# GpSimd's subtraction for the weights' low parts, cut from one instruction per tile into four

## The chip, the cores and the metric

The kernel runs on one core of one Trainium2 chip. The metric is the device time of one execution in microseconds (us). Before the change it is 1412.34 us, the median of three runs (1410.88 to 1412.73).

A core has five engines that run side by side and wait for each other by semaphores: TensorE (PE in the profile; PEld is its weight load), VectorE (DVE), ScalarE (ACT), GpSimd (POOL) and SyncE (SP), which only issues transfers here.

## The reference

256 positions of 1024 channels pass through three transformer layers. Cut to the products that matter here:

```python
# layer 1
mod = silu(c) @ ada_w + ada_b
proj = (rmsnorm(x) * (1 + sc1) + sh1) @ w_in          # 1024 x 3624
mix = concat([hgrn2_mixer(..), dsa_mixer(..), conv_module(..)]) @ w_out
x = x + g1 * mix
ff = square(relu(h @ mlp_w1)) @ mlp_w2                # 1024 x 4096, 4096 x 1024
x = rmsnorm(x + g2 * ff)
# layers 2 and 3
x = layer_norm(ALPHA * x + mixer(x))                  # MLA and stick-breaking, then "fox"
x = layer_norm(ALPHA * x + (silu(x @ w1) * (x @ w3)) @ w2)   # inner width 2816
x = x + sigmoid(x @ ple_w_gate + b) * (p @ ple_w_proj)
```

All data are float32.

## The kernel before

**Weights as a stream.** Every weight matrix is cut on the host into tiles of at most 128 x 2048 (1 MB), in the order in which TensorE uses them (`STREAM`). SyncE loads them into a ring of three buffers, `raw`. The 24 tiles `ada*` are multiplied as they are (line 569). Each of the other 159 (`SPLIT`) is made into two rounded parts, so that a float32 product is three fast ones:

- ScalarE copies `raw` to `w_hi` in the rounded type (line 949, inside `ahead`, called two tiles ahead between its other work). There are three `w_hi` buffers.
- GpSimd subtracts: `w_lo = raw - w_hi` (line 1279, inside `remainder`). There are two `w_lo` buffers. 155 of the tiles have 2048 columns; the others have 1088, 256, 1536 and 128.
- TensorE's `product3` (lines 491, 496 and 497) adds `a_hi*b_hi`, `a_hi*b_lo` and `a_lo*b_hi` in PSUM.

The activations are split in the same way by VectorE: at the start of a stage `split_input` makes `hT_hi` (a cast, line 1344) and `hT_lo` (a subtraction, line 1345), in four chunks of 512 columns; in the first MLP lines 1677 to 1679 square, cast and subtract each half of the hidden layer, and in the two later ones lines 1882 to 1887 do two multiplications, a cast and a subtraction per pair of tiles.

**Who waits for whom.** GpSimd starts tile n when ScalarE has rounded it and TensorE has finished the first product of tile n-1, since only then is the `w_lo` buffer of tile n-2 free:

```python
pool.wait_ge(weights_rounded, n + 1)
if n >= LO:
    pool.wait_ge(weights_started, n - LO + 2)
```

TensorE waits for the whole tile (`pe.wait_ge(weights_split, n + 1)` in `tile`) before its first product of it. So GpSimd cannot work ahead: from one tile's first product to the next tile's first product there must be time for one whole subtraction. The same semaphore, `weights_split`, lets SyncE overwrite the `raw` buffer.

**Stages.** A product with 1024 inputs takes one tile for 256 outputs: 48 products of 256 columns (`feature_half`, `token_half`). The down projections (`down`, 16 tiles in the first MLP, 11 in each of the other two) have 24 products of 512 columns per tile. The first MLP's up projection has 16 tiles (`m1`), the two others 22 each (`f13`, two tiles per step). In the stage of the gated recurrence (VectorE's lines 1498 to 1529, eight levels) GpSimd also computes a convolution of 31 taps, each a multiplication (line 1290) and an addition (line 1292) of 512 columns, with a wait behind each, and puts the subtractions of four tiles between the first taps; from the last instruction of such a tile to the next tap's multiplication there is no wait.

At the end of the layers 2 and 3 comes the stage with the embedding product (`pp`) and the gate products (`pg`).

Of the kernel before, what the change touches and what calls it, by code (L numbers as in the profile page):

```python
# [23 lines left out]
F32 = mybir.dt.float32  # L24
ALU = mybir.AluOpType
# [9 lines left out]
RAW, HI, LO = 3, 3, 2  # L35
# [43 lines left out]
def width(name):  # L79
    return WIDTH.get(name, TILE)  # L80
# [175 lines left out]
def bank(*key):  # L256
    return USE[key] % BANKS


def read(*key):  # L260

    return USE[key] // BANKS + 1


def build(nc, x_in, wstream, pcol_in, prow_in, const_in, p_in, out):
    ctx = ExitStack()
    with ctx:
        def sb(name, shape):
            return ctx.enter_context(nc.sbuf_tensor(name, shape, F32))

        def sem(name):
            return ctx.enter_context(nc.semaphore(name))
# [6 lines left out]
        def rounded(name, n, offset=None):  # L279

            if offset is None:
                return ctx.enter_context(nc.sbuf_tensor(name, [P, n], F32R))
            return nc.alloc_sbuf_tensor_at(name, [P, n], F32R, offset=arena_at + 4 * offset)

        raw = sb("raw", [P, RAW, TILE])
        w_hi = [rounded(f"w_hi{i}", TILE) for i in range(HI)]
        w_lo = [rounded(f"w_lo{i}", TILE) for i in range(LO)]
# [25 lines left out]
        def col(name, i=0, n=1):  # L313
            return pcol[:, PCOL[name] + i:PCOL[name] + i + n]
# [90 lines left out]
        weights_split = sem("weights_split")  # L405
# [40 lines left out]
        @block.sync  # L446
        def _(sp):
            for i, name in enumerate(STREAM):
                if i >= RAW:
                    before = STREAM[i - RAW]  # L450
                    if before in SPLIT_NO:
                        sp.wait_ge(weights_split, SPLIT_NO[before] + 1)
                    elif int(before[3:]) % 2 == 0:
                        sp.wait_ge(ada_used, int(before[3:]) // 2 + 1)
                    else:
                        sp.wait_ge(psum_full, full("mod", int(before[3:]) // 2))
                sp.dma_start(raw[:, i % RAW, 0:width(name)], wstream[i, :, 0:width(name)])\
                    .then_inc(weights_loaded[i % RAW], 16)
            sp.wait_ge(x_done, 1)
            sp.dma_start(out.rearrange("o (t p) d -> p (o t) d", p=P), x[:, :, :])\  # L460
                .then_inc(out_stored, 16)
            sp.wait_ge(out_stored, 16)
# [800 lines left out]
        @block.gpsimd  # L1263
        def _(pool):
            step = [0]

            def link(ins):
                step[0] += 1
                ins.then_inc(pool_step, 1)
                pool.wait_ge(pool_step, step[0])  # L1270

            def remainder(name):

                n, slot = SPLIT_NO[name], TILE_NO[name]
                pool.wait_ge(weights_rounded, n + 1)
                if n >= LO:
                    pool.wait_ge(weights_started, n - LO + 2)
                m = width(name)
                nc.gpsimd.tensor_tensor(w_lo[n % LO][:, 0:m], raw[:, slot % RAW, 0:m],  # L1279
                                        w_hi[n % HI][:, 0:m].bitcast(F32), ALU.subtract).then_inc(weights_split, 1)  # L1280

            hp = hpad.rearrange("p (c n) -> p c n", c=2)
            acc = conv.rearrange("p (c n) -> p c n", c=2)

            def tap(j):


                product_ = mixT[:, 4 + 2 * (j % 2):6 + 2 * (j % 2), :]
                w = col("cv_w", 2 * j, 2).unsqueeze(2).to_broadcast([P, 2, T])
                link(nc.gpsimd.tensor_tensor(product_, hp[:, :, j:j + T], w, ALU.mult))  # L1290
                before = col("cv_b", 0, 2).unsqueeze(2).to_broadcast([P, 2, T]) if j == 0 else acc
                last = nc.gpsimd.tensor_tensor(acc, product_, before, ALU.add)
                if j < 30:
                    link(last)
                else:
                    last.then_inc(conv_done, 1)

            for name in SPLIT[:SPLIT_NO["hg.0"]]:
                remainder(name)
            pool.wait_ge(pcol_loaded, 16)  # L1300
            pool.wait_ge(bank_read[bank("cu", 0)], read("cu", 0))
            for j in range(31):
                tap(j)

                if j % 2 == 0 and SPLIT_NO["hg.0"] + j // 2 < SPLIT_NO["wo0.0"]:
                    remainder(SPLIT[SPLIT_NO["hg.0"] + j // 2])
            for name in SPLIT[SPLIT_NO["wo0.0"]:]:
                remainder(name)
# [738 lines left out]
```

## Time and profile before

| | |
|---|---|
| median of three runs | 1412.34 us (1410.88 to 1412.73) |
| span of the profiled execution, first to last instruction | 1405.2 us |
| median less that span | 7.1 us |
| TensorE, busy share | 85% |
| VectorE, busy share | 52% |
| ScalarE, busy share | 37% |
| GpSimd, busy share | 58% |
| line 1279: 159 instructions, busy | 731.3 us |
| mean granted TensorE clock | 0.918 of full speed |

"Busy" includes time in which an instruction has started and is held up. The times of the profiled execution are given from the start of its span; of its own time the profile has the span alone, so the work around it is read from the median.

### The profile page before, as it was taken

Reading aid. Unit: us, or ns where it says so; the run is one execution under the profiler, and the core shown is the slowest. Engines: PE = TensorE matmul, PEld = TensorE weight load, DVE = VectorE, ACT = ScalarE, POOL = GpSimd, SP = SyncE. Lnnn points to the kernel's source line nnn. Section 1 sums busy time; section 2 is a strip of 40 time slices with the busy share of each in tenths; the row PEclk is TensorE's granted clock in tenths of the full one; section 3 lists DMA queues with packets and bytes.
Section 4 is the critical chain, followed back from the end, with each engine's and each line's share of the span. In section 5 each row is a group of like instructions: output and inputs, shape, how many; then the busy total and the mean of one; then the engine's idle time right before and its main releaser. Section 6 shows DMA issues by size and latency. Waiting matters only on the chain.

```text
span 1405.2 us, 18835 instructions
## 1 busy us (share of the span) xinstructions
PE 1200.8 (85%) x8000; PEld 1104.7 (79%) x8000; DVE 727.2 (52%) x778; ACT 521.1 (37%) x672; POOL 813.5 (58%) x225
## 2 busy tenths in 40 slices
PE   6699769576999996975779999976999788999976
PEld 5699658466998885973679999866987488999866
DVE  2396999656999005336555553074022536555054
ACT  1453210433343333456433333333554433333341
POOL 0476896133877882740157878844743146888863
PEclk9899879868999997997799999988999889999998
DMA  9442218412444554330034455524432033455540
GB/s 363 167 175 90 91 36 302 172 44 106 164 167 174 185 183 161 139 129 1 31 120 150 181 180 182 207 92 165 181 120 90 0 120 130 191 186 184 181 148 30
DMA packets 28131, 200.95 MB, mean 143 GB/s; under 512 B 3089, under 2 KB 3473, under 8 KB 4881
## 3 DMA queue, kind: packets, MB, share of 16 engines
q1 hardware_dynamic: 26624, 190.30, 37.0%
q10 hardware_dynamic: 1424, 9.46, 1.8%
q8 instruction: 63, 1.03, 0.3%
q14 instruction: 20, 0.16, 0.0%
HBM read 198.70 MB, written 1.05 MB: 142 GB/s over the span
## 4 chain that ended last, share of the span: by engine, by line
PE 68%; DVE 20%; ACT 5%; issue 4%; DMA 1%; POOL 1%; DVEq 0%; ACTq 0%; POOLq 0%
PE bank L491 19%; PE bank L496 18%; PE bank L497 18%; PE bank L569 6%; DVE hT_hi L1344 4%; DVE hT_lo L1345 3%; DVE arena L1677 2%; PE bank L620 2%; DVE hid_lo L1679 2%; DVE arena L1529 1%; PE bank L613 1%; DVE hid_hi L1678 1%; PE bank L857 1%; PE bank L856 1%; POOL w_lo L1279 1%
## 5 line engine op out<-in xcount | busy, mean ns | idle before, releaser
L1279 POOL TENSOR_TENSOR w_lo<-raw,w_hi 128x2048 fp32r<-128x2048 f32 (+1 forms) x159 | 731.3, 4600 | 569.6 <-PE bank L491 489.2
L949 ACT ACTIVATE w_hi<-raw 128x2048 fp32r<-128x2048 f32 (+1 forms) x159 | 299.6, 1886 | 342.1 <-PE bank L491 288.2
L491 PE MATMUL bank<-hT_hi,w_hi 128*128 128x256 f32 (+1 forms) x1360 | 392.1, 288 | 35.1 <-DVE hT_lo L1345 30.1
L496 PE MATMUL bank<-hT_lo,w_hi 128*128 128x256 f32 (+1 forms) x1360 | 389.3, 286 | 0.0
L497 PE MATMUL bank<-hT_hi,w_lo 128*128 128x256 f32 (+1 forms) x1360 | 389.1, 286 | 0.0
L491 PEld LDWEIGHTS bank<-hT_hi,w_hi 128*128 128x128 f32 (+1 forms) x1360 | 264.3, 194 | 39.7 <-DVE hT_lo L1345 20.3
L496 PEld LDWEIGHTS bank<-hT_lo,w_hi 128*128 128x128 f32 (+1 forms) x1360 | 264.2, 194 | 0.2
L497 PEld LDWEIGHTS bank<-hT_hi,w_lo 128*128 128x128 f32 (+1 forms) x1360 | 263.7, 194 | 0.3
L491 PE MATMUL bank<-w_hi,hT_hi 128*128 128x256 f32 (+2 forms) x544 | 164.5, 302 | 35.0 <-DVE hT_lo L1345 29.0
L496 PE MATMUL bank<-w_lo,hT_hi 128*128 128x256 f32 (+2 forms) x544 | 161.8, 298 | 0.0
L497 PE MATMUL bank<-w_hi,hT_lo 128*128 128x256 f32 (+2 forms) x544 | 161.7, 297 | 0.0
L491 PEld LDWEIGHTS bank<-w_hi,hT_hi 128*128 128x128 f32 x544 | 113.5, 209 | 39.3 <-DVE hT_lo L1345 25.2
L491 PE MATMUL bank<-w_hi,hid_hi 128*128 128x512 f32 (+1 forms) x336 | 128.9, 384 | 1.8 <-POOL w_lo L1279 1.8
L496 PE MATMUL bank<-w_lo,hid_hi 128*128 128x512 f32 (+1 forms) x336 | 128.7, 383 | 0.0
L497 PE MATMUL bank<-w_hi,hid_lo 128*128 128x512 f32 (+1 forms) x336 | 128.5, 383 | 0.0
L496 PEld LDWEIGHTS bank<-w_lo,hT_hi 128*128 128x128 f32 x544 | 113.7, 209 | 0.2
L497 PEld LDWEIGHTS bank<-w_hi,hT_lo 128*128 128x128 f32 x544 | 113.4, 208 | 0.2
L569 PE MATMUL bank<-raw,tiny 128*128 128x256 f32 x384 | 88.0, 393 | 10.6 <-DVE tiny L1449 9.0
L1886 DVE CAST hid_hi<-arena 128x512 fp32r<-128x512 f32 x22 | 96.0, 4366 | 0.7
L569 PEld LDWEIGHTS bank<-raw,tiny 128*128 128x128 f32 x384 | 75.9, 198 | 22.6 <-DVE tiny L1449 9.0
L491 PEld LDWEIGHTS bank<-w_hi,hid_hi 128*128 128x128 f32 x336 | 64.4, 192 | 14.3 <-POOL w_lo L1279 2.3
L497 PEld LDWEIGHTS bank<-w_hi,hid_lo 128*128 128x128 f32 x336 | 64.2, 191 | 12.0
(242 smaller groups left out, 1347.0 us busy)
## 6 DMA issues: line engine op xcount, KB each, us to landing
raw<-wstream SPq DMA_DIRECT2D x179, 1024.0 KB, 4.8
arena<-prow ACTq DMA_DIRECT2D x2, 2560.0 KB, 8.9
x_res<-x ACTq DMA_DIRECT2D x1, 1024.0 KB, 12.4
rows<-prow ACTq DMA_DIRECT2D x2, 512.0 KB, 15.4
out<-x_res SPq DMA_DIRECT2D x1, 1024.0 KB, 4.0
const_sb<-const ACTq DMA_DIRECT2D x1, 936.0 KB, 14.2
raw<-wstream SPq DMA_DIRECT2D x1, 768.0 KB, 4.1
raw<-wstream SPq DMA_DIRECT2D x1, 544.0 KB, 3.6
```

Of the source, the lines that this page charges most:

```text
L491: ins = mm(o, a[0], b[0], start=start, stop=False)
L496: mm(o, a[0], b[1], start=False, stop=False)
L497: return mm(o, a[1], b[0], start=False, stop=stop)
L569: last = mm(b[:, j * T:(j + 1) * T], csil[:, k:k + 1].to_broadcast([P, P]), w[:, k, :], start=k == 0, stop=k == DC - 1)
L620: last = mm(b[par * 64:par * 64 + 64, hh * P:(hh + 1) * P], values(4 * g + par + 2 * hh, m), pT_[:, (hh * nb + m) * P:(hh * nb + m + 1) * ...
L949: A(w_hi[n % HI][:, 0:m], raw[:, slot % RAW, 0:m], ACT.Copy).then_inc(weights_rounded, 1)
L1279: nc.gpsimd.tensor_tensor(w_lo[n % LO][:, 0:m], raw[:, slot % RAW, 0:m], w_hi[n % HI][:, 0:m].bitcast(F32), ALU.subtract).then_inc(weights ...
L1344: link(V.tensor_copy(hT_hi[:, s], src))
L1345: V.tensor_tensor(hT_lo[:, s], src, hT_hi[:, s].bitcast(F32), ALU.subtract).then_inc(input_split, 1)
L1677: link(V.tensor_tensor(v, act_out[n % 2], act_out[n % 2], ALU.mult))
L1679: V.tensor_tensor(hid_lo[:, hs], v, hid_hi[:, hs].bitcast(F32), ALU.subtract).then_inc(hid_split, 1)
L1886: link(V.tensor_copy(hid2_hi[:, hs], v))
```

## The change

In `remainder` the one subtraction of a tile becomes a loop. The step is 512 columns where the width is a multiple of 512, and a quarter of the width otherwise: four instructions per tile, but three of 512 for the one tile of 1536 columns. The four follow each other with no wait between them. The two waits stand before the first, and the semaphore `weights_split` is raised by the last. The tile's data and all other engines' instructions are the same. The line of the subtraction becomes 1281, and those below it move on by three.

```diff
                 m = width(name)
-                nc.gpsimd.tensor_tensor(w_lo[n % LO][:, 0:m], raw[:, slot % RAW, 0:m],
-                                        w_hi[n % HI][:, 0:m].bitcast(F32), ALU.subtract).then_inc(weights_split, 1)
+                step_ = 512 if m % 512 == 0 else m // 4
+                for c in range(0, m, step_):
+                    last = nc.gpsimd.tensor_tensor(w_lo[n % LO][:, c:c + step_], raw[:, slot % RAW, c:c + step_],
+                                                   w_hi[n % HI][:, c:c + step_].bitcast(F32), ALU.subtract)
+                last.then_inc(weights_split, 1)
```

## Rows read from the trace of the kernel before

**Rows 1.** The page: busy time of each engine, and the chain by engine.
```profile
PE 1200.8 (85%) x8000; PEld 1104.7 (79%) x8000; DVE 727.2 (52%) x778; ACT 521.1 (37%) x672; POOL 813.5 (58%) x225
...
PE 68%; DVE 20%; ACT 5%; issue 4%; DMA 1%; POOL 1%; DVEq 0%; ACTq 0%; POOLq 0%
```

**Rows 2.** Busy time by stretch: an up projection (f13), then its down projection.
```profile
core 0: us, PE busy (x) PEld busy (x) DVE busy (x) ACT busy (x) POOL busy (x), PEclk, DMA share, GB/s
735.00:870.00 135.00, 135.00 (x1083) 133.34 (x1083) 75.29 (x48) 49.40 (x34) 105.35 (x23) 0.99 0.49 178
870.00:922.00 52.00, 50.45 (x223) 41.43 (x221) 3.38 (x6) 18.75 (x11) 42.66 (x10) 1.00 0.52 185
```

**Rows 3.** Timeline of GpSimd: narrower tiles, and two tiles of a down projection.
```profile
start us, us, engine line op out<-in xcount [idle before <-releaser]
600.61 3.52 POOL L1279 TENSOR_TENSOR w_lo<-raw,w_hi 128x1536 fp32r<-128x1536 f32 x1 [1.14 <-PE bank L491]
...
960.48 0.46 POOL L1279 TENSOR_TENSOR w_lo<-raw,w_hi 128x128 fp32r<-128x128 f32 x1 [1.14 <-PE bank L491]
...
871.85 4.62 POOL L1279 TENSOR_TENSOR w_lo<-raw,w_hi 128x2048 fp32r<-128x2048 f32 x1 [0.81 <-PE bank L491]
877.31 4.62 POOL L1279 TENSOR_TENSOR w_lo<-raw,w_hi 128x2048 fp32r<-128x2048 f32 x1 [0.84 <-PE bank L491]
```

**Rows 4.** Timeline of GpSimd between tiles and taps, and VectorE beside it.
```profile
125.86 4.59 POOL L1279 TENSOR_TENSOR w_lo<-raw,w_hi 128x2048 fp32r<-128x2048 f32 x1
130.41 1.04 POOL L1290 TENSOR_TENSOR mixT<-arena,pcol_sb 128x512 f32<-128x512 f32 x1
...
136.08 4.89 POOL L1279 TENSOR_TENSOR w_lo<-raw,w_hi 128x2048 fp32r<-128x2048 f32 x1
140.91 1.50 POOL L1290 TENSOR_TENSOR mixT<-arena,pcol_sb 128x512 f32<-128x512 f32 x1
...
202.58 1.27 POOL L1292 TENSOR_TENSOR arena<-mixT,arena 128x512 f32<-128x512 f32 x1
...
136.40 5.12 DVE L1529 TENSOR_TENSOR arena<-arena 128x512 f32<-128x512 f32 x1
141.56 1.41 DVE L1498 TENSOR_TENSOR xn<-arena 128x512 f32<-128x512 f32 x1
```

**Rows 5.** Timeline of GpSimd and VectorE in the first up projection (m1).
```profile
355.57 5.08 POOL L1279 TENSOR_TENSOR w_lo<-raw,w_hi 128x2048 fp32r<-128x2048 f32 x1 [1.14 <-PE bank L491]
...
392.31 4.59 POOL L1279 TENSOR_TENSOR w_lo<-raw,w_hi 128x2048 fp32r<-128x2048 f32 x1 [3.12 <-ACT w_hi L949]
397.49 4.91 POOL L1279 TENSOR_TENSOR w_lo<-raw,w_hi 128x2048 fp32r<-128x2048 f32 x1 [0.59 <-PE bank L491]
...
355.48 0.69 DVE L1679 TENSOR_TENSOR hid_lo<-arena,hid_hi 128x512 fp32r<-128x512 f32 x1
356.21 5.00 DVE L1677 TENSOR_TENSOR arena<-arena 128x512 f32<-128x512 f32 x1
```

**Rows 6.** Waits of TensorE, 345 to 470 us: in total, times, longest.
```profile
PE bank L491 <- POOL w_lo L1279: 5.5, 4, 1.8
```

**Rows 7.** Timeline of GpSimd and VectorE in an up projection f13.
```profile
745.62 4.63 POOL L1279 TENSOR_TENSOR w_lo<-raw,w_hi 128x2048 fp32r<-128x2048 f32 x1 [1.14 <-PE bank L491]
...
746.18 4.34 DVE L1886 CAST hid_hi<-arena 128x512 fp32r<-128x512 f32 x1
750.56 0.69 DVE L1887 TENSOR_TENSOR hid_lo<-arena,hid_hi 128x512 fp32r<-128x512 f32 x1
```

**Rows 8.** Timeline of VectorE in the first input product, and in the residual behind the mixer.
```profile
87.76 3.44 DVE L1479 TENSOR_TENSOR arena<-arena 128x1024 f32<-128x1024 f32 x1 [0.69 <-ACT arena L1025]
91.24 9.05 DVE L1482 TENSOR_TENSOR_SCAN xn<-ones,arena 128x256 f32<-128x256 f32 x4
...
309.35 4.54 DVE L1662 TENSOR_TENSOR x_res<-x_res,arena 128x512 f32<-128x512 f32 x1
```

**Rows 9.** Timeline at the start of the up projection m1: GpSimd, then VectorE.
```profile
337.12 4.73 POOL L1279 TENSOR_TENSOR w_lo<-raw,w_hi 128x2048 fp32r<-128x2048 f32 x1 [12.27 <-PE bank L491]
...
337.50 4.63 DVE L1344 CAST hT_hi<-arena 128x512 fp32r<-128x512 f32 x1
...
343.35 0.69 DVE L1345 TENSOR_TENSOR hT_lo<-arena,hT_hi 128x512 fp32r<-128x512 f32 x1
```

**Rows 10.** Timeline at the start of layer 2's gate stage: GpSimd, VectorE, TensorE.
```profile
930.57 5.06 POOL L1279 TENSOR_TENSOR w_lo<-raw,w_hi 128x2048 fp32r<-128x2048 f32 x1 [10.55 <-PE bank L491]
936.74 4.76 POOL L1279 TENSOR_TENSOR w_lo<-raw,w_hi 128x2048 fp32r<-128x2048 f32 x1 [1.11 <-PE bank L491]
...
937.13 4.92 DVE L1345 TENSOR_TENSOR hT_lo<-arena,hT_hi 128x512 fp32r<-128x512 f32 x1
...
942.11 0.58 PE L491 MATMUL bank<-w_hi,hT_hi 128*128 128x256 f32 x1 [3.48 <-DVE hT_lo L1345]
```

## The prediction

> **What bounds the kernel now.** I read the busy times and the chain first, then stretches, then single rows. TensorE is busy 85% of the span and carries 68% of the chain that ended last; VectorE carries 20%, GpSimd 1% [rows 1]. In the up projections TensorE is never idle, and GpSimd is busy 105 of 135 us beside it; in the down projections it is close to the same [rows 2]. That "1%" is deceptive. GpSimd may not work ahead: tile n's subtraction starts behind the first product of tile n-1 and must end before tile n's. What matters is the room in that loop. In a down projection a tile comes about every 5.44 us: the subtraction takes 4.62 and GpSimd idles 0.81 [rows 3]; in the wide products tiles come every 5.76 us (4.62 busy and 1.14 idle) [rows 5, 7]. How much of the idle time is room? At 397.49 us TensorE itself had waited for GpSimd, and still GpSimd was idle 0.59 us [rows 5]: that is the loop's own latency (the end of the subtraction, the first product, the next start). So the real room is 1.14 - 0.59 = **0.55 us** per tile in wide products and about **0.2 us** in down projections.
>
> The second thing to see is that GpSimd and VectorE hold each other up. A cast of 512 columns takes 4.34 us when a subtraction of GpSimd started before it [rows 7], a two-input operation of 0.69 us takes 5.00, and a subtraction that starts while VectorE's is running takes 5.08 instead of 4.62 [rows 5]. One of them has to end before the other goes on. The blocked VectorE operation that began at 356.21 ends at 361.21, 0.56 after GpSimd's end at 360.65, so its 0.69 began 0.13 before that end; the other way round GpSimd loses 0.46. I take 0.14 us of overlap at each exchange.
>
> The Trainium skill (SBUF — State Buffer, "Who interferes with whom") calls this an exclusive lock, taken for a whole instruction by GpSimd or by a VectorE operation that has two SBUF inputs or uses both ports. The trace agrees (5.00 against 0.69).
>
> **Cost of a piece.** 128 columns take 0.46 us, 1536 take 3.52 and 2048 take 4.62 [rows 3]. That is 2.15 to 2.17 ns a column over a fixed 0.19, which gives 1.29 us for 512 columns; the convolution's addition of 512 columns takes 1.27 [rows 4]. I take 1.28. Of two instructions with no wait between them the second starts about 0.045 us before the first ends (125.86 + 4.59 = 130.45 against 130.41) [rows 4]. Four pieces take 4 x 1.28 - 3 x 0.045 = **4.99 us**, 0.37 more than now. Bounds: nothing is added if a piece's fixed part vanishes behind its neighbour (1.15, a quarter of 4.62), and 1.32 a piece if the slope from the 1536-column tile is carried down.
>
> On that price the Trainium skill (GPSIMD Engine Reference, "Performance pitfalls for Q7 kernels") speaks against the change: a read command costs about 102 cycles that do not overlap with the previous one. As an estimate, three more instructions with one to two such reads are 0.26 to 0.51 us a tile, 4.88 to 5.13 in all; by the upper one the result would be some 9 us later than mine. No row here shows it apart.
>
> **Does VectorE get in between pieces?** At 140.91 GpSimd's tap follows the tile at once. A VectorE subtraction was waiting and got in: it ended at 141.52, and the tap took 1.50 us instead of 1.04. At 130.41, with nobody waiting, the same tap took 1.04 [rows 4]. So yes, by the nearest row, at the end of every instruction. A two-input operation in a gap costs GpSimd 0.46, a cast (0.43 us) 0.43 - 0.28 + 0.045 = 0.20.
>
> **The sum, where it costs:**
> - Down projections: 4.99 + 0.60 = 5.59 us per tile against 5.44. Some 35 intervals (15 + 10 + 10) x 0.15 = **+5.3**.
> - f13: in every second tile a cast and a subtraction now enter between the pieces: 4.99 + 0.20 + 0.46 = 5.65, and with 0.59 a period of 6.24 against 5.76. Nothing can be made up, as GpSimd can't work ahead. 22 steps x 0.48 = **+10.6**. The other tile of each step (4.99 + 0.59 = 5.58) still fits.
> - m1: three operations per tile (0.46, 0.20, 0.46). When TensorE falls behind, the first of them lands in the 0.59 between two tiles, wholly or partly, so a tile takes 5.65 to 6.1 and the period is 6.24 to 6.7; I take 6.37. 16 x 0.61 = 9.8. Against it stands what m1 loses now: VectorE, blocked for a whole tile at a time, falls behind, ScalarE then rounds late (3.12 us of idle at 392.31 [rows 5]), and TensorE waits 5.5 us [rows 6]. That wait goes. Together **+4.3**.
> - First input product: the subtraction of 1024 columns and the four scans [rows 8] enter between pieces of three tiles, some 0.8 over the period each, an estimate from 0.46 apiece: **+2.5**.
> - Residual behind the mixer: three tiles with one operation each [rows 8], 4.99 + 0.46 + 0.59 - 5.76 = 0.28: **+0.9**.
>
> **Where it pays:**
> - Gate stages, twice. VectorE's last subtraction waits behind the second tile until 942.05, and TensorE 3.48 us for it [rows 10]. Now the first tile really starts at 931.0 (5.06 - 4.62 late); its pieces alternate with cast, subtraction, cast: 4 x 1.28 + 1.55 - 6 x 0.14 = 5.83, end at 936.85; the last subtraction ends at 937.4. The wait of 3.48 goes, but TensorE gets the tile 0.6 later than now: 2 x 2.9 = **-5.8**.
> - Other stage starts, eight. The cast is blocked for 4.2 us, but behind it stand three more operations, and all of them alternate with pieces now. From the real start at 337.23: 5.83 + 0.55 gives 343.6 for the last, against 344.04 now [rows 9]. 8 x 0.4 = **-3.2**. So the most visible stalls give back next to nothing.
> - Recurrence: VectorE's work at 136.40 is blocked 4.4 us [rows 4], and there are four such tiles, at most 4 x 3.3 = 13. But each tile ends some 1.8 us later, and the products hg.1 and hi.1 and the exponentials behind them are waited for. Taking the order through piece by piece with the prices above leaves **-3**; the bounds are 0 and -10.
>
> Everything that only unblocks VectorE elsewhere costs and gives nothing, as TensorE covers it; without that cover VectorE's operations would count. The loads cost nothing: a `raw` buffer comes free at the end of its subtraction, as now, just before the tile's first product, so its reload keeps a whole period.
>
> Sum: 5.3 + 10.6 + 4.3 + 2.5 + 0.9 - 5.8 - 3.2 - 3.0 = **+11.6 us**. The sum is made against the profiled span of 1405.2, which gives 1416.8; with the 7.1 us between that span and the median (an unprofiled 1412.34) that is **1424 us**.
>
> **Rivals.**
> - *Pieces are nearly free and the stalls shrink* (faster). If GpSimd prepares a piece while the one before streams, four take about 4.65. Down projections then lose nothing, f13 0.5 in all, m1 is even, the first product loses 1.5, the residual nothing, and the gains of 12 stay: -10, **1402**. It decides below about 1.245 us a piece. For it: the overlap of 0.045 shows some preparation. Against: the fixed 0.19 is still in the tap behind a tile. Chance 0.19.
> - *The ends cancel*, with pieces of 1.24 to 1.26: **1412**, chance 0.08.
> - *GpSimd keeps its place through its four pieces.* Then VectorE is blocked for 4.99 instead of 4.62: down +5.3, m1 +7.5 (VectorE falls further behind), stage starts and recurrence 10 x 0.37 = 3.7 and no gains: about +16, **1428**. Against: the row at 140.91. Chance 0.12.
> - *A piece costs over 1.35*, since dispatch shows between short instructions. At 1.40, a tile takes 5.47 + 0.59 = 6.06, and all of about 100 wide tiles run late: +0.3 each, the mixed ones and the down projections more: some +53, **1465**. No row of 512 columns is that long unblocked. Chance 0.05.
> - *The forecast itself*, 0.56.
>
> **The numbers.** A measurement of this kernel can tell about 0.2% (2.8 us) from no change. Faster takes the first rival, 0.19; within 0.2% 0.09, the cancelling case and an edge; slower the rest, 0.72. With 1.25 a piece the sum is some +2, with 1.32 some +21. The range, 1405 to 1436 us, leaves out the far end of the dispatch case and the lower part of the first rival.
>
> **What would show it.** 512-column pieces of 1.27 to 1.29 us, starts 1.24 apart; down projections with periods near 5.59; f13 periods of 5.76 and 6.2 in turn, and waits of TensorE for GpSimd of some 0.5 us there; in m1 the late rounding gone; VectorE's longest operations near 1.7 us instead of 5; the 3.48 us before the gate product gone. Wrong: periods of 5.44 in the down projections (pieces cheaper), or VectorE's casts still over 4 us (no entry between pieces).

## The result and the profile after

The changed kernel takes **1440.26 us** (median of 4 runs, 1439.02 to 1445.19) against 1412.53 for the kernel before beside it (4 runs, 1410.88 to 1413.70): a ratio of 1.0208, 95% interval 1.0188 to 1.0228. A second measurement in the study gave 1442.93 against 1407.22, ratio 1.0243 (1.0218 to 1.0268). The forecast was 1424, with a range up to 1436: the sign was right and the size was not. The change costs 28 to 36 us where the sum had 11.6. The ratios are estimated apart from the medians, with their intervals, and can differ slightly from the ratio of two medians.

The profiled execution took 1445.19 us, its span 1443.4, and TensorE's mean granted clock was 0.911 of full speed (0.918 before). First the page of the changed kernel: the busy times and the chain by engine, as [rows 1].

```profile
PE 1234.3 (86%) x8000; PEld 1112.6 (77%) x8000; DVE 599.6 (42%) x778; ACT 526.6 (36%) x672; POOL 930.8 (64%) x701
...
PE 57%; POOL 24%; DVE 11%; ACT 4%; issue 2%; DMA 1%; DVEq 0%; POOLq 0%; ACTq 0%
```

VectorE's busy time fell by 127.6 us, because it is blocked less, and GpSimd's rose by 117.3. On the chain GpSimd went from 1% to 24% and VectorE from 20% to 11%. VectorE was freed, and GpSimd became what TensorE waits for. The stretches that answer to [rows 2] (up projection f13, then its down projection):

```profile
core 0: us, PE busy (x) PEld busy (x) DVE busy (x) ACT busy (x) POOL busy (x), PEclk, DMA share, GB/s
752.00:887.00 135.00, 131.83 (x1046) 128.11 (x1046) 44.94 (x44) 50.30 (x34) 119.76 (x90) 1.00 0.46 166
887.00:939.00 52.00, 51.97 (x219) 40.07 (x218) 0.00 (x0) 17.55 (x10) 45.69 (x37) 1.00 0.51 185
```

In 135 us TensorE now does 1046 products instead of 1083, and in the 52 us of the down projection 219 instead of 223, with GpSimd busy 45.69 us where it was 42.66.

Now the places of the sum, in the program's order. Timeline of GpSimd in the first input product; then at the start of m1 (GpSimd, then VectorE), as [rows 9]; then in m1 (GpSimd, then VectorE), as [rows 5]:

```profile
start us, us, engine line op out<-in xcount [idle before <-releaser]
88.16 6.54 POOL L1281 TENSOR_TENSOR w_lo<-raw,w_hi 128x512 fp32r<-128x512 f32 x4 [0.59 <-PE bank L491]
95.28 6.92 POOL L1281 TENSOR_TENSOR w_lo<-raw,w_hi 128x512 fp32r<-128x512 f32 x4 [0.59 <-PE bank L491]
...
339.37 6.01 POOL L1281 TENSOR_TENSOR w_lo<-raw,w_hi 128x512 fp32r<-128x512 f32 x4 [11.36 <-PE bank L491]
...
339.77 1.40 DVE L1347 CAST hT_hi<-arena 128x512 fp32r<-128x512 f32 x1
344.30 1.64 DVE L1348 TENSOR_TENSOR hT_lo<-arena,hT_hi 128x512 fp32r<-128x512 f32 x1
...
358.27 5.76 POOL L1281 TENSOR_TENSOR w_lo<-raw,w_hi 128x512 fp32r<-128x512 f32 x4 [0.59 <-PE bank L491]
364.62 6.08 POOL L1281 TENSOR_TENSOR w_lo<-raw,w_hi 128x512 fp32r<-128x512 f32 x4 [0.59 <-PE bank L491]
...
358.52 1.41 DVE L1681 CAST hid_hi<-arena 128x512 fp32r<-128x512 f32 x1
359.97 1.67 DVE L1682 TENSOR_TENSOR hid_lo<-arena,hid_hi 128x512 fp32r<-128x512 f32 x1
```

A row with x4 is a whole tile. VectorE's casts and two-input operations of 512 columns that were held up for 4.3 to 5.0 us [rows 5, 7, 9] now take 1.40 (a cast) or 1.64 to 1.67 (two inputs): they wait for one piece. And each one that gets in makes the tile longer, with GpSimd idle just 0.59 us around it, so that the loop itself sets the pace.

Timeline of GpSimd in an up projection f13, as [rows 7], and in its down projection, as [rows 3]:

```profile
758.55 5.67 POOL L1281 TENSOR_TENSOR w_lo<-raw,w_hi 128x512 fp32r<-128x512 f32 x4 [0.70 <-PE bank L491]
764.81 5.06 POOL L1281 TENSOR_TENSOR w_lo<-raw,w_hi 128x512 fp32r<-128x512 f32 x4 [0.59 <-PE bank L491]
...
885.40 5.05 POOL L1281 TENSOR_TENSOR w_lo<-raw,w_hi 128x512 fp32r<-128x512 f32 x4 [0.70 <-PE bank L491]
891.16 5.04 POOL L1281 TENSOR_TENSOR w_lo<-raw,w_hi 128x512 fp32r<-128x512 f32 x4 [0.71 <-PE bank L491]
```

The f13 tiles start 6.26 and 5.76 us apart in turn. In the down projection the tile's four pieces take 5.04 and the starts are 5.76 apart, not 5.59: the idle time is 0.70, where 0.60 was forecast. TensorE's own rows at the change of tile say why:

```profile
890.12 0.39 PE L497 MATMUL bank<-w_hi,hid_lo 128*128 128x512 f32 x1
890.50 0.50 PE L491 MATMUL bank<-w_hi,hid_hi 128*128 128x512 f32 x1
890.85 0.40 PE L496 MATMUL bank<-w_lo,hid_hi 128*128 128x512 f32 x1
```

Products of one tile start 0.23 us apart and take 0.39. The first product of a tile that TensorE had to wait for takes 0.50, and GpSimd may start on the next tile only behind it (it does at 891.16). The 0.59 of [rows 5] was read behind a late first product of 256 columns, in the kernel before:

```profile
396.96 0.39 PE L491 MATMUL bank<-hT_hi,w_hi 128*128 128x256 f32 x1 [1.34 <-POOL w_lo L1279]
```

That product takes 0.39 us, so the loop is 0.11 us longer with products of 512 columns.

Last, layer 2's gate stage (GpSimd, VectorE, TensorE), as [rows 10]:

```profile
952.34 6.29 POOL L1281 TENSOR_TENSOR w_lo<-raw,w_hi 128x512 fp32r<-128x512 f32 x4 [10.16 <-PE bank L491]
959.23 9.02 POOL L1281 TENSOR_TENSOR w_lo<-raw,w_hi 128x512 fp32r<-128x512 f32 x4 [0.59 <-PE bank L491]
...
959.22 3.47 DVE L1762 TENSOR_TENSOR x_res<-xn,arena 128x1024 f32<-128x1024 f32 x2
962.72 4.40 DVE L1765 TENSOR_TENSOR x_res<-x_res,arena 128x1024 f32<-128x1024 f32 x2
...
968.30 0.58 PE L491 MATMUL bank<-w_hi,hT_hi 128*128 128x256 f32 x1 [3.59 <-POOL w_lo L1281]
```

The wait of 3.48 us for VectorE is gone, as forecast, and a wait of 3.59 for GpSimd stands in its place, one tile later. Behind VectorE's last subtraction stand four residual updates of 1024 columns. TensorE's next products don't need them, but they get in between the pieces of the second tile and stretch it to 9.02 us.

**Stages.** The times below lie between the same ScalarE instructions in each trace, as a mean of two traces of the kernel before and two of the changed one (spans 1405.2 and 1411.0, 1443.4 and 1441.0; means 34.1 us apart).

| stage | forecast, us | measured, us |
|---|---|---|
| to the end of the first input product | +2.5 | +5.4 |
| recurrence, on to the output product of the mixer | -3.0 | -4.8 |
| that product and the start of m1 | +0.1 | -0.5 |
| m1 and its down projection | +6.6 | +9.1 |
| layer 2's mixer, to its first f13 step | -1.2 | +0.8 |
| layer 2's f13 and down projection | +6.8 | +8.8 |
| layer 2's gate stage, to layer 3's attention | -3.3 | +1.2 |
| layer 3's attention | 0 | +3.8 |
| from there to its first f13 step | -0.8 | +0.9 |
| layer 3's f13 and down projection | +6.8 | +9.1 |
| last gate stage to the end | -2.9 | +0.3 |
| sum | +11.6 | +34.1 |

The smallest of these differences are within what two traces of one kernel show: those of the kernel before lie 2.7 us apart in layer 2's mixer, and those of the change 3.1 us in the first input product (3.8 and 7.0 more than before).

### The profile page after: what moved, and what is told of

Same layout as the page of the kernel before. It is cut to its first block, busy times and chain, and to the rows that moved or that the text cites. A ratio compares the mean times of both kernels' runs of the same rounds, so it can differ in the third digit from the quotient of the medians.

```text
span 1443.4 us, 19311 instructions
## 1 busy us (share of the span) xinstructions
PE 1234.3 (86%) x8000; PEld 1112.6 (77%) x8000; DVE 599.6 (42%) x778; ACT 526.6 (36%) x672; POOL 930.8 (64%) x701
## 3 DMA queue, kind: packets, MB, share of 16 engines
q10 hardware_dynamic: 1424, 9.46, 1.7%
## 4 chain that ended last, share of the span: by engine, by line
PE 57%; POOL 24%; DVE 11%; ACT 4%; issue 2%; DMA 1%; DVEq 0%; POOLq 0%; ACTq 0%
POOL w_lo L1281 23%; PE bank L491 16%; PE bank L496 14%; PE bank L497 14%; PE bank L569 5%; DVE hT_lo L1348 3%; DVE hT_hi L1347 2%; PE bank L620 2%; PE bank L857 1%; PE bank L613 1%; PE bank L856 1%; DMA raw<-wstream 1%; PE bank L555 1%; POOL arena L1295 1%; POOL mixT L1293 1%
## 5 line engine op out<-in xcount | busy, mean ns | idle before, releaser
L1281 POOL TENSOR_TENSOR w_lo<-raw,w_hi 128x512 fp32r<-128x512 f32 x635 | 851.0, 1372 | 490.9 <-PE bank L491 427.0
L491 PE MATMUL bank<-hT_hi,w_hi 128*128 128x256 f32 (+1 forms) x1360 | 398.9, 293 | 44.0 <-DVE hT_lo L1348 26.8
L491 PE MATMUL bank<-w_hi,hid_hi 128*128 128x512 f32 (+1 forms) x336 | 132.7, 395 | 3.1 <-POOL w_lo L1281 3.0
L496 PEld LDWEIGHTS bank<-w_lo,hid_hi 128*128 128x128 f32 x336 | 63.7, 190 | 10.7
```

The source lines that it names most:

```text
L491: ins = mm(o, a[0], b[0], start=start, stop=False)
L496: mm(o, a[0], b[1], start=False, stop=False)
L1281: last = nc.gpsimd.tensor_tensor(w_lo[n % LO][:, c:c + step_], raw[:, slot % RAW, c:c + step_], w_hi[n % HI][:, c:c + step_].bitcast(F32), ...
```

## The experiments

In those that cut, the form is that of the change, and only the tiles that are cut and the widths differ. `COND` and `STEPS` are given with each; a tile outside `COND` keeps its one instruction.

```diff
-                nc.gpsimd.tensor_tensor(w_lo[n % LO][:, 0:m], ...).then_inc(weights_split, 1)
+                steps = STEPS if COND else [m]
+                c = 0
+                for s_ in steps:
+                    last = nc.gpsimd.tensor_tensor(w_lo[n % LO][:, c:c + s_], ...)
+                    c += s_
+                last.then_inc(weights_split, 1)
```

### The change by parts

**Down projections alone**, in pieces of 512:

```diff
+                COND: name[:2] in ('m2', 'f2')
```

> Only the 38 tiles of the down projections (m2, f2) are cut into four. VectorE works on nothing there, so this is the price of the cuts alone. Theory A (a piece has a fixed cost, and GpSimd's loop has no room): a tile takes 5.04 us instead of 4.62 and the period goes from 5.44 to 5.74, 38 x 0.30 = +11 us over the kernel before. Theory B (the cuts are nearly free and the 28 us come from VectorE's entries between pieces): within 2 us of the kernel before. Theory C (a lower granted clock makes the loss): no change of the period, and whatever is lost shows as a lower clock.

1420.52 us (1417.38 to 1425.27), ratio 1.0096 (1.0076 to 1.0117). Timeline of GpSimd in a down projection of this kernel:

```profile
890.07 5.04 POOL L1282 TENSOR_TENSOR w_lo<-raw,w_hi 128x512 fp32r<-128x512 f32 x4 [0.71 <-PE bank L491]
895.81 5.04 POOL L1282 TENSOR_TENSOR w_lo<-raw,w_hi 128x512 fp32r<-128x512 f32 x4 [0.70 <-PE bank L491]
```

VectorE does next to nothing in these stages, so this is the pure price of the cuts: a period of 5.74 us against 5.44 to 5.46, and +3.3, +3.7 and +3.7 us in the three down projections. That is 10.7 in all, some 0.30 for each of the 35 intervals, twice the forecast's 5.3.

**Up projections alone**, m1 and f13:

```diff
+                COND: name[:2] == 'm1' or name[:3] == 'f13'
```

> Only the 60 tiles of the up projections (m1, f13) are cut into four. Theory A: m1 periods of 6.54 us against 5.76, 16 x 0.78 = 12.5, less the 5.5 us that TensorE waits there now; f13 0.52 per step, 22 x 0.52 = 11.4; together +18 us. Theory B: the same, and it is then nearly all of the loss (over +24 us). Theory C: under +5 us.

1433.82 us (1422.46 to 1437.42), ratio 1.0169 (1.0133 to 1.0205). Its f13 tiles behave as in the whole change (ten intervals in 119.82 us against 119.81, and 115.20 before), so the two kinds of projection don't depend on each other there. m1 and its down projection take just 2.7 us more than before, where 7 were expected.

**All the others alone:**

```diff
+                COND: not (name[:2] in ('m1', 'm2', 'f2') or name[:3] == 'f13')
```

> The other 61 tiles alone are cut into four: the first input products, the tiles among the convolution's taps, the mixers' products and the gate stages. By the two traces: +6.9 us up to 112 us, -4.6 in the recurrence, -0.6 behind it, +1.6 in the two gate stages, some +0.6 elsewhere: +2 to +6 us. If the parts add up (theory A), the three runs sum to the 28 us of the whole change; if they don't, there is a loss that only the whole has. The prediction had a gain of 6.6 us for this part.

1418.39 us (1415.21 to 1420.57), ratio 1.0076 (1.0057 to 1.0096). Here lie all the places that should have paid back. Of these the recurrence does (144.4 us against 149.2), but the first input product takes nearly as much again (115.7 against 111.7).

The three ratios make 1.034 together, the change 1.021 to 1.024. Much of the difference lies in layer 3's attention, to which the study comes back below. With that stage taken out of each profiled span, the kernel before has 1378.6 us (mean of its two traces), and the parts 1391.3, 1394.5 and 1380.5, which is 12.7, 15.9 and 1.9 more and 30.5 in sum; the change has 1408.9 (mean of two), 30.3 more. So the totals add up, but not every stage does. m1 and its down projection take 3.3, 2.7 and -1.2 us more in the three runs, 4.8 in sum, and 9.1 more in the whole change. The starts of GpSimd's tiles show a part of it. From the down projection's second tile to the first tile behind it there are fifteen intervals. They take 85.4 us in the kernel before, because ScalarE's late rounding reaches into its first tiles, and 81.8 when m1 alone is cut, because that lateness is gone. With the down projection cut they take 87.3 us behind a late m1 (alone) and 86.8 behind a punctual one (the whole change). So the same cut costs 1.9 us in the one case and 5.0 in the other. What makes up for it in the other stages wasn't taken apart.

**Both kernels again**, with no edit to either, on the chip of the next two runs:

> The kernel before, once more, for a second profiled execution. The two traces at hand differ by 5.9 us in the attention of layer 3, where GpSimd has no tile in hand, and the granted clock there was 0.61 and 0.54 in the slices of the changed kernel and 1.00 in those of the kernel before. If that fall belongs to the executions and not to the change (theory D), this trace may show it too, and its stages other than that one agree with the first trace within 1 us. If it belongs to the change (theory C), the clock stays at 1.00 here, as before.

> The changed kernel, once more. Theory D: the stages with tiles lose what they lost in the first trace, +32 us without that attention stage, within 2 us, and the attention stage anything from 0 to +13. In the median against the kernel before: +25 to +32 us.

1407.76 us for the kernel before (ratio 1.0005, 0.9988 to 1.0023), and 1442.93 for the change. The first says that two measurements of one kernel agree within 0.3%; the second that the loss of 2 per cent and more stands on another chip too.

### Is it the cut, or who enters?

In f13 VectorE's cast and subtraction fall on every second tile. Cutting only those, or only the other ones, keeps the number of extra instructions and changes whether anybody gets in.

```diff
+                COND: name[:3] == 'f13' and name[-2:] == '.1'
```

> Only those 22 tiles of f13 are cut into four (the .1 of each step) that GpSimd subtracts while VectorE casts and subtracts. Theory A: a cut tile with two entries takes 5.7 us and the loop 0.59, so each step is 0.5 longer: +11 us over the two stages, read between the first and the last sigmoid of each. Theory B' (the price is in the cuts and not in the entries): about what f13_quiet costs.

```diff
+                COND: name[:3] == 'f13' and name[-2:] == '.0'
```

> Only the other 22 tiles of f13 (the .0 of each step) are cut into four; VectorE does nothing there that holds GpSimd up. Theory A: 5.05 us a tile and 0.6 to 0.7 of loop is 5.65 to 5.75 and still fits into 5.76, so the two stages take as long as before, within 0.5 us. Theory B': some of f13_met's loss.

Timeline of GpSimd in f13, the tiles cut where VectorE enters:

```profile
755.11 5.67 POOL L1282 TENSOR_TENSOR w_lo<-raw,w_hi 128x512 fp32r<-128x512 f32 x4 [1.11 <-PE bank L491]
761.38 4.63 POOL L1282 TENSOR_TENSOR w_lo<-raw,w_hi 128x2048 fp32r<-128x2048 f32 x1 [0.59 <-PE bank L491]
```

And with the quiet ones cut:

```profile
755.05 5.06 POOL L1282 TENSOR_TENSOR w_lo<-raw,w_hi 128x512 fp32r<-128x512 f32 x4 [1.13 <-PE bank L491]
760.81 4.62 POOL L1282 TENSOR_TENSOR w_lo<-raw,w_hi 128x2048 fp32r<-128x2048 f32 x1 [0.70 <-PE bank L491]
```

A quiet cut tile takes 5.06 and its start is still 5.76 us from the next: the cut is paid from the idle time, and ten intervals take 115.20 us, as before; the kernel takes 1410.97 (ratio 1.0015, 0.9999 to 1.0030). A tile that is entered takes 5.67, its successor starts 6.27 later, and the ten intervals take 119.80, which is 0.51 for each of nine late steps (TensorE meets the first one with time in hand). The kernel takes 1424.07 (ratio 1.0114, 1.0090 to 1.0138). Without layer 3's attention its span is 10.4 us longer than that of the kernel before, about what the two stages f13 lose. So in f13 the cost is the entry, 5.67 - 5.06 = 0.61 us for a cast and a subtraction, of which 0.51 shows. The forecast had 0.66 and 0.48. The cut of the other tiles adds nothing there, but without the cut nobody could get in.

### Fewer pieces

```diff
+                COND: True, STEPS: [m // 2] * 2
```

> Every tile is cut into two instead of four. Theory A puts a threshold between the two: two pieces of 2.4 us are 4.75 us a tile, and with 0.6 to 0.7 of loop that is 5.35 to 5.45 in the down projections, where the room is 5.44; with one entry of VectorE 5.2 + 0.6 in f13, about the 5.76 there. So the down projections and f13 lose under 1 us each, m1 loses less of its waits for late roundings, and the whole is between -8 and +4 us. If the loss goes by the number of extra instructions (a third of the change's), +9 us.

1413.91 us against 1411.72, ratio 1.0017 (1.0005 to 1.0029). Timeline of GpSimd in a down projection, then in f13:

```profile
880.62 4.76 POOL L1282 TENSOR_TENSOR w_lo<-raw,w_hi 128x1024 fp32r<-128x1024 f32 x2 [0.72 <-PE bank L491]
886.11 4.76 POOL L1282 TENSOR_TENSOR w_lo<-raw,w_hi 128x1024 fp32r<-128x1024 f32 x2 [0.72 <-PE bank L491]
...
743.24 4.95 POOL L1282 TENSOR_TENSOR w_lo<-raw,w_hi 128x1024 fp32r<-128x1024 f32 x2 [0.98 <-PE bank L491]
749.00 4.78 POOL L1282 TENSOR_TENSOR w_lo<-raw,w_hi 128x1024 fp32r<-128x1024 f32 x2 [0.81 <-PE bank L491]
```

One more instruction costs 4.76 - 4.62 = **0.14 us**, three cost 0.42. At 0.14 the down projection's period is 5.49 (0.5 us in the whole of a stage f2), and in f13 every tile still fits into 5.76 us. The price of the change is thus a matter of degree. With the loop's 0.70 the room in a down projection is 5.44 - 4.62 - 0.70 = 0.12 us, not the 0.2 of the prediction: one extra instruction (0.14) overruns it slightly, three (0.42) by 0.30. In f13 the 0.55 us hold three extra instructions, but not with a cast and a subtraction of VectorE besides (0.42 + 0.61).

### The gate stage

```diff
+                COND: name[:2] == 'pg'
```

> Only the eight tiles of the gate products (pg) are cut into four. The prediction gave 5.8 us back here. By the traces the wait of 3.48 us before the gate product goes, but the four 1024-column updates of the residual then enter the second tile, which takes 9.02 us, and TensorE waits 3.6 us for that: the two stages within 2 us of the kernel before, together.

1421.64 us (1403.92 to 1425.64), ratio 1.0038 (1.0009 to 1.0067). Timelines of GpSimd and of TensorE:

```profile
929.38 6.30 POOL L1282 TENSOR_TENSOR w_lo<-raw,w_hi 128x512 fp32r<-128x512 f32 x4 [10.55 <-PE bank L491]
936.27 9.02 POOL L1282 TENSOR_TENSOR w_lo<-raw,w_hi 128x512 fp32r<-128x512 f32 x4 [0.58 <-PE bank L491]
...
945.35 0.58 PE L491 MATMUL bank<-w_hi,hT_hi 128*128 128x256 f32 x1 [3.59 <-POOL w_lo L1282]
```

These are the durations of the whole change to 0.01 us: what goes wrong in this stage is made in it. From ScalarE's table load at line 920 to its last sigmoid of line 1255, the two gate stages take 1.0 and 1.1 us more than in the mean of the two traces of the kernel before, where the forecast had 2.9 less for each. The difference between the medians is thus mostly not theirs: in this trace layer 3's attention takes 38.5 us, against 27.8 and 31.3 in those of the kernel before. To let VectorE's last subtraction in, but not the residual updates, only the second tile was cut, and only once, behind its first 256 columns:

```diff
+                COND: name in ('pg0_0.1', 'pg1_0.1'), STEPS: [256, m - 256]
```

> Of the gate products only the second tile of each stage (pg0_0.1, pg1_0.1) is cut, into 256 and 1792 columns. VectorE's last subtraction enters behind 0.75 us, and the updates of the residual stay behind the long piece. If the entry of the updates is what takes the gain away, it is there now: -3.4 us in each stage, -7 in all. If the gain isn't there for another reason, 0.

1421.98 us (1408.31 to 1424.15), ratio 1.0056 (1.0031 to 1.0081). VectorE, then GpSimd, then TensorE in the same stage:

```profile
935.16 1.27 DVE L1350 TENSOR_TENSOR hT_lo<-arena,hT_hi 128x512 fp32r<-128x512 f32 x1
936.47 10.54 DVE L1764 TENSOR_TENSOR x_res<-xn,arena 128x1024 f32<-128x1024 f32 x2
...
952.67 4.50 POOL L1282 TENSOR_TENSOR w_lo<-raw,w_hi 128x2048 fp32r<-128x2048 f32 x1 [6.74 <-ACT w_hi L949]
...
957.22 0.41 PE L491 MATMUL bank<-w_hi,hT_hi 128*128 128x256 f32 x1 [5.03 <-POOL w_lo L1282]
```

The subtraction does get in (1.27 us instead of 4.92 [rows 10]). Then the first two residual updates are held up for 10.54 us by this tile and the next. VectorE comes late to the bank that it has to read, ScalarE rounds late, GpSimd idles 6.74 us for it, and TensorE waits 5.03. The two gate stages take 1.3 us more each, measured as above, where 3.4 less were expected. The reading is that this stage has an amount of work on VectorE and GpSimd that can't overlap, and that cutting picks which of it is late; no run shows that amount by itself.

### The opposite: GpSimd waits

At a stage start TensorE needs VectorE's eight operations at once and GpSimd's second tile only later. If exclusion is the trouble, GpSimd should hold back there, with its instruction whole:

```diff
+                hold = {"hf.1": 4, "wo0.1": 8, "m1_0.1": 12, "cqkv.1": 16, "o0_0.1": 22, "f13_0_0.1": 26,
+                        "fq0.0": 34, "o1_0.1": 38, "f13_1_0.1": 42, "pg0_0.0": 30, "pg1_0.0": 46}
+                if name in hold:
+                    pool.wait_ge(input_split, hold[name])
```

> The kernel before with its uncut subtractions, but at eleven stage starts GpSimd waits until VectorE has made all chunks of the input split before it begins the subtraction of the stage's second tile. It tests whether the block of about 4.2 us at each stage start lies on the path. If it does: the last chunk comes 4 us sooner at nine starts, -25 to -36 us in all, less what the late subtraction costs TensorE in the two gate stages (1 to 2 us each). If TensorE is held by something else there (the late second tile), between -5 and +10 us.

**1373.24 us** (1371.40 to 1374.63), ratio **0.9755** (0.9735 to 0.9775): 34 us faster than the kernel before (1407.86 beside it), and some 67 faster than the change. At the start of m1, GpSimd, VectorE and TensorE of this kernel:

```profile
332.40 4.59 POOL L1283 TENSOR_TENSOR w_lo<-raw,w_hi 128x2048 fp32r<-128x2048 f32 x1 [15.14 <-DVE hT_lo L1349]
...
327.51 0.43 DVE L1348 CAST hT_hi<-arena 128x512 fp32r<-128x512 f32 x1 [2.33 <-ACT arena L934]
329.89 0.43 DVE L1348 CAST hT_hi<-arena 128x512 fp32r<-128x512 f32 x1
...
332.29 0.39 PE L491 MATMUL bank<-hT_hi,w_hi 128*128 128x256 f32 x1 [0.21 <-DVE hT_lo L1349]
332.51 0.28 PE L496 MATMUL bank<-hT_lo,w_hi 128*128 128x256 f32 x1
```

The kernel before has in that place, in TensorE's timeline:

```profile
342.92 0.58 PE L491 MATMUL bank<-hT_hi,w_hi 128*128 128x256 f32 x1 [4.41 <-DVE hT_lo L1345]
```

The wait falls from 4.41 to 0.21 us. A part of the gain is TensorE's clock: behind the long wait the granted clock is 0.50 in the window 343 to 346 us of the kernel before, and its next product takes 0.42 us; behind the short one it is 1.00 in the window 332 to 335 us, and the product takes 0.28. Seven stage starts get 4.5 to 5.8 us shorter (m1's from 22.3 to 16.5), the two up projections f13 each lose 3.6 again (118.8 us for the ten intervals instead of 115.2). There TensorE waits 1.8 us for the late second tile, and behind this wait its granted clock is 0.50 and 0.70 in the windows 713 to 715 and 715 to 717 us. The gate stages gain 1.2 to 1.4 each.

The same without the gate entries, with the single cut of the gate tile and with m1 in halves:

```diff
-                        "fq0.0": 34, "o1_0.1": 38, "f13_1_0.1": 42, "pg0_0.0": 30, "pg1_0.0": 46}
+                        "fq0.0": 34, "o1_0.1": 38, "f13_1_0.1": 42}
+                COND: name in ('pg0_0.1', 'pg1_0.1') or name[:2] == 'm1'
+                STEPS: [256, m - 256] for pg, [m // 2] * 2 for m1
```

> The waits of 'hold' at nine stage starts (without the two gate stages), the cut of 'gate_first' in the gate stages, and m1's tiles cut into two. Theory A: -34 us as in 'hold', -3 more from the gate stages (-7 in place of about -4), and in m1 up to -4 as VectorE gets in between the halves and ScalarE's roundings are no longer late: about -40 us, 1368 us. If m1's halves cost more than they give: -33 to -36.

1378.56 us (1376.10 to 1378.76), ratio 0.9763 (0.9747 to 0.9778). m1 and its down projection take 183.63 us against 183.83 with whole tiles: halves gain nothing there. Nothing of the cutting adds to the waiting: without layer 3's attention the two spans are 1341.2 and 1340.7 us, and the ratios 0.9763 and 0.9755 can't be told apart.

### Layer 3's attention: the clock

This stage has no tile of GpSimd and the same instructions in every kernel. TensorE's windows in it, of the kernel before, of the change, and of the one with f13's entered tiles cut:

```profile
core 0: us, PE busy (x), PEclk, DMA share, GB/s
1097.00:1105.00 8.00, 8.00 (x46) 1.00 0.01 2
```
```profile
core 0: us, PE busy (x), PEclk, DMA share, GB/s
1119.00:1127.00 8.00, 8.00 (x31) 0.61 0.01 2
1127.00:1135.00 8.00, 8.00 (x21) 0.54 0.00 0
```
```profile
core 0: us, PE busy (x), PEclk, DMA share, GB/s
1108.00:1116.00 8.00, 8.00 (x23) 0.50 0.00 0
1116.00:1124.00 8.00, 8.00 (x23) 0.50 0.00 0
```

In these windows TensorE is busy all the time, but at a granted clock of 1.00, of 0.54 to 0.61, or of 0.50, the 1.2 GHz level, and it does half as many products at 0.50 as at 1.00. Over the whole stage the mean granted clock is 0.97, 0.79 and 0.63 in the three, and TensorE is busy for 24.0 of 27.8 us, 29.5 of 33.3 and 35.4 of 38.5. The stage takes 27.8 us at best and 38.5 at worst:

| kernel | stage, us |
|---|---|
| before; down projections alone | 27.8; 27.9 |
| before, again; quiet f13 tiles; the eleven waits | 31.3; 31.4; 31.4 |
| halves; the gate tile cut once; the change, twice | 33.1; 33.3; 33.3 and 33.3 |
| waits and cuts together; all the others | 35.5; 35.7 |
| entered f13 tiles; up projections; gate stage in four | 38.5; 38.5; 38.5 |

So up to 10.7 us hang on something other than the work. The kernel before itself shows two values. The cutting of the gate stage falls into two groups of runs, 1403.92 to 1413.91 and 1421.31 to 1425.64 us, the single cut of the gate tile into 1408.31 to 1414.31 and 1421.83 to 1424.15, and the cutting of the up projections into 1422 to 1424 and 1433 to 1437. The groups are some 11 us apart, about as far as the stage's best and worst. Only one execution of each was profiled, so that the groups are made in this stage isn't shown. It would explain why the ratios of the parts don't add. What decides the level at that point isn't settled: it isn't told by which tiles are cut, and no run here changed only when the stage begins.

## Why the prediction was right and wrong

- **VectorE gets in between pieces: right.** Casts of 1.40 and two-input operations of 1.67 us in place of 4.3 to 5.0, and the rival in which GpSimd keeps its place has fallen. The Trainium skill (SBUF — State Buffer, "Who interferes with whom") has the exclusion for one instruction; the trace adds that it is handed over even between two GpSimd instructions with nothing to wait for.
- **The price of a piece: right.** 5.04 us for four where 4.99 was taken, so the rival of nearly free pieces has fallen, and so has that of 1.40 a piece. The Trainium skill (GPSIMD Engine Reference, "Performance pitfalls for Q7 kernels") led to an estimate of 0.26 to 0.51 us for three more instructions. Measured are 0.42, inside it; that read commands make up this time is shown by no run.
- **Down projections, +5.3: mis-sized by a factor of 2.** The step that failed is "4.99 + 0.60 = 5.59". The 0.60 came from products of 256 columns [rows 5], whose first one behind a wait takes 0.39; with products of 512 columns it takes 0.50, and the loop 0.70. With 5.04 + 0.70 = 5.74 the term is +10.7, and the run that cut nothing else shows it. Some 0.05 of the missing 0.15 per tile are the pieces, 0.10 the loop. A loop's latency was read in one stage and used in another.
- **f13, +10.6: right.** 0.51 a step against 0.48, and by the pair of runs for the reason given.
- **m1, +4.3: mis-sized.** From its third tile's start to that of the down projection's second, fifteen intervals, it takes 98.1 us instead of 90.9, which is +7.2. The mean period is 6.54 against the 6.37 taken, 2.7 over 16 tiles. The late rounding did go, but of the 5.5 us of waits only 4.5 (90.9 - 15 x 5.76) lay in these intervals.
- **First input product, +2.5: mis-sized.** It cost 5.4. The periods are 7.12 and 7.50 around the tiles shown and 6.2 in the two before, together 4.0 over 5.76 each. VectorE's operations ahead of the subtraction and the two-input operations behind the scans enter too and weren't counted. The other 1.4 weren't taken apart.
- **Residual behind the mixer, +0.9: no visible cost.** That stage and the start of m1 became 0.5 shorter together, and the start alone is 0.5 shorter, where 0.4 was forecast ("the most visible stalls give back next to nothing").
- **Gate stages, -5.8: wrong.** The step that failed is "the wait of 3.48 goes": it went and came back as 3.59 for the second tile, and the stages with what follows them cost 1.2 and 0.3 instead of paying. The working followed the operations that TensorE waits for, and stopped there. Those behind them in VectorE's queue, four of 1024 columns, now enter too.
- **Recurrence, -3: right in kind**, -4.8 measured.
- **Layer 3's attention: not foreseen**, +3.8 in the means, and left open.
- **The base.** The prediction put 7.1 us around the span. In all the runs a kernel's time is 1.8 to 2.2 us above its span, and two traces of the kernel before have spans of 1405.2 and 1411.0. So some 5 of the 7.1 were probably the distance of one quick execution from the median; of the 5.8 between those two spans 3.5 lie in the attention stage. With the mean of the two spans the same sum would have come to 1421.6.

By the table, the 22.5 us between forecast and measurement are: gate stages 7.7, the three pairs of projections 6.8, attention's clock 3.8, the mixers of layers 2 and 3 together 3.7, the first input product 2.9, less 2.4 for the recurrence and the start of m1. The 3.7 weren't taken apart.

## What to carry to other kernels

Where two engines exclude each other, cutting the long instruction lets the other in between the pieces, with everything in its queue and not only what someone waits for; so list what stands behind the urgent operation before counting a wait as gone. Measure the room of a loop in the stage itself, since the loop's latency depends on the products in it, and compare the extra instructions with that room: here one cost next to nothing (1.0017 in the whole), three did not fit. If work is blocked at a stage's start by an engine that is not yet needed, let that engine wait instead: that gave 2.4% where cutting lost 2.

## What the hardware showed that was not expected

- The first product of a tile that TensorE had to wait for takes 0.50 us instead of 0.39 (512 columns, full clock), and of 256 columns 0.39 instead of 0.28.
- An extra GpSimd instruction over the same columns costs 0.14 us, whether one or three are added.
- TensorE's granted clock in a stage of small products goes from 1.00 to 0.50 between kernels, and partly between executions of one kernel, with the same instructions: 27.8 to 38.5 us for a stage in which TensorE is busy for 86 to 92% of the time.
